# Two transformer blocks on one core: modulation on VectorE in 512-column operations, and another order of loads

## The reference, cut to what matters

```
c_act = jax.nn.silu(c)                                  # one row of 1024
for l in range(2):
    mod = c_act @ w_ada[l] + b_ada[l]                   # 1024 x 3072 weights, one row
    shift, scale, gate = split_cols(mod, (D, D, D))
    h = rms_norm(x, g_pre[l]) * (1.0 + scale) + shift
    (...) = split_cols(h @ w_in[l], IN_SPLITS)          # 1024 x 7328 weights
    # three attentions (8 + 8 + 4x2 heads), gates, output projections: y
    x = x + gate * rms_norm(y, g_post[l])
```

## Time and profile before

| | us |
|---|---|
| median of 3 runs (lowest to highest) | 2483.28 (2481.02 to 2483.42) |
| the profiled execution's own time | 2480.68 |
| its span | 2478.9 |
| TensorE matmul busy | 2309.0 (93%) |
| VectorE busy | 1462.6 (59%) |
| ScalarE busy | 1164.0 (47%) |
| GpSimd busy | 116.6 (5%) |

### The profile page before, as it was taken

How to read it: one execution, slowest core, us unless ns; L and a number is a source line. 1 busy time by engine, 2 the same in 40 slices (tenths; PEclk the granted TensorE clock), 3 DMA queues, 4 the chain that set the end, 5 groups by cost and what they waited for, 6 DMA issues and landing times.

```text
span 2478.9 us, 30332 instructions
## 1 busy us (share of the span) xinstructions
PE 2309.0 (93%) x11596; PEld 1931.6 (78%) x11596; DVE 1462.6 (59%) x1778; ACT 1164.0 (47%) x1416; POOL 116.6 (5%) x61
## 2 busy tenths in 40 slices
PE   6899998889999989999887789999999999999998
PEld 5687677768777878899886668787878787878786
DVE  4311455220145366555543279888888888888886
ACT  0211232121133046443453157777777777767775
POOL 0203322000000012000000000000000000000000
PEclk9999999989999989999898889999999999999999
DMA  9546433444322353355340669998999899999991
GB/s 290 136 137 203 136 103 121 122 102 152 103 85 85 120 156 113 129 194 180 120 148 1 248 219 364 327 367 323 368 324 367 323 371 325 357 339 357 342 351 43
DMA packets 348640, 536.22 MB, mean 216 GB/s; under 512 B 51084, under 2 KB 195392, under 8 KB 348552
## 3 DMA queue, kind: packets, MB, share of 16 engines
q1 hardware_dynamic: 342848, 530.29, 62.3%
q10 hardware_dynamic: 5704, 4.71, 0.6%
HBM read 533.89 MB, written 1.07 MB: 216 GB/s over the span
## 4 chain that ended last, share of the span: by engine, by line
PE 87%; DVE 7%; ACT 3%; issue 1%; DMA 1%; ACTq 0%; POOL 0%; DVEq 0%; SPq 0%
PE bank L561 22%; PE bank L590 17%; PE bank L592 16%; PE bank L591 16%; PE bank L722 2%; PE bank L569 1%; DVE rstd L1733 1%; PE bank L583 1%; PE bank L1107 1%; PE bank L1099 1%; PE bank L651 1%; PE bank L1142 1%; PE bank L686 1%; PE bank L688 1%; PE bank L704 1%
## 5 line engine op out<-in xcount | busy, mean ns | idle before, releaser
L2200 DVE TENSOR_TENSOR w_lo<-pool,w_hi 128x2048 fp32r<-128x2048 f32 x336 | 765.7, 2292 | 134.7 <-ACT w_hi L1622 134.6
L1622 ACT ACTIVATE w_hi<-pool 128x2048 fp32r<-128x2048 f32 x336 | 643.1, 1917 | 147.9 <-PE bank L592 146.3
L561 PE MATMUL bank<-h,ring 128*128 128x256 f32 (+1 forms) x1968 | 448.3, 387 | 11.0 <-DVE h L1835 6.5
L561 PEld LDWEIGHTS bank<-h,ring 128*128 128x128 f32 (+1 forms) x1968 | 373.7, 192 | 81.8 <-issue 24.4
L590 PE MATMUL bank<-w_hi,xe_hi 128*128 128x512 f32 x896 | 359.7, 401 | 4.3 <-DVE w_lo L2200 4.3
L592 PE MATMUL bank<-w_hi,xe_lo 128*128 128x512 f32 x896 | 350.4, 391 | 0.0
L591 PE MATMUL bank<-w_lo,xe_hi 128*128 128x512 f32 x896 | 350.0, 391 | 0.0
L1904 DVE TENSOR_TENSOR piece_lo<-ring,piece_hi 128x1024 fp32r<-128x1024 f32 x118 | 145.2, 1237 | 112.6 <-ACT piece_hi L1263 112.5
L590 PE MATMUL bank<-left_hi,piece_hi 128*128 128x256 f32 x672 | 197.5, 294 | 9.9 <-DVE left_lo L1909 6.2
L590 PEld LDWEIGHTS bank<-w_hi,xe_hi 128*128 128x128 f32 x896 | 168.8, 188 | 45.3 <-DVE w_lo L2200 10.4
L592 PEld LDWEIGHTS bank<-w_hi,xe_lo 128*128 128x128 f32 x896 | 168.7, 188 | 36.3
(11 more groups left out here) (351 smaller groups left out, 2886.7 us busy)
## 6 DMA issues: line engine op xcount, KB each, us to landing
pool<-in_od_exp_w SPq DMA_DIRECT2D x336, 1024.0 KB, 7.0
ring<-in_w_in SPq DMA_DIRECT2D x52, 1024.0 KB, 5.2
ring<-in_ev_ffn_w SPq DMA_DIRECT2D x33, 1024.0 KB, 5.2
ring<-in_w_ada SPq DMA_DIRECT2D x24, 1024.0 KB, 8.4
ring<-in_od_w_in SPq DMA_DIRECT2D x12, 1024.0 KB, 5.4
ring<-in_ev_w_in SPq DMA_DIRECT2D x10, 1024.0 KB, 5.4
ring<-in_w_out SPq DMA_DIRECT2D x8, 1024.0 KB, 5.1
ring<-in_w_in SPq DMA_DIRECT2D x16, 256.0 KB, 4.5
```

What stands on the lines that cost most here:

```text
L561: m = nc.tensor.matmul(b[base:base + rows, 0:cols], left(k), right(k), start=(k == 0), stop=(k == K - 1))
L1622: nc.scalar.activation(w_hi[q % 3], ring_slot(q), ACT.Copy)\
L2200: V.tensor_tensor(w_lo[q % 3], ring_slot(q), w_hi[q % 3].bitcast(F32), ALU.subtract).then_inc(item_vector, tick(item_vector, "lo", q))
```

## The change

- GpSimd computes no modulation any more. `modulation_direct` remains for one unit, (0, 3). The other eleven are VectorE's. It takes both items of a unit in one operation of 2 x 256 = 512 columns where they lie in neighbouring slots of the ring; where they don't (slots 5 and 0), it stays at 256 columns. Each operation waits for the one before it, whose sums it adds to.
- The list begins with units 0, 3, 1, 2 of layer 0 (shift and scale, eight items). The gate units of layer 0 and all of layer 1 lie among layer 0's projections, two items each.
- SyncE no longer waits for the small vectors; identity is fetched ahead of x and has a semaphore of its own.
- ScalarE issues the fetches of biases and tables after the root of layer 0's mean square. Bias lines, lambdas and the bias table's twelve products move in among the projections, on all engines.
- In layer 0, h is x times 1/rms first, then times gain plus shift in one operation.

```diff
-    ADA_ORDER, ADA_VECTOR = (0, 4, 1, 5, 2, 3), 4
-    ADA_AFTER = ("za1", "qb", "zb", "qc")
-    ADA_UNIT = {1: 1, 7: 2, 13: 3, 19: 4}
+    ADA_FIRST, ADA_MATMUL = (0, 3, 1, 2), 3
+    ADA_LATER = [("ckv", 0, 4), ("za1", 0, 5), ("qb1", 1, 0), ("kvb", 1, 1), ("zb1", 1, 2), ("qc1", 1, 3),
+                 ("kc1", 1, 4), ("vc1", 1, 5)]
+    ADA_UNITS = [(0, 0), (0, 1), (0, 2)] + [(l, i) for _, l, i in ADA_LATER]
...
+        pe.wait_ge(consts_set, when(consts_set, "mean"))
+        mean_square(("pre", 0), KD, 1024)
         pe.wait_ge(vecs_ready, when(vecs_ready, "c_act"))
-        modulation_direct(0, 4)
-        pe.wait_ge(loaded_bias, when(loaded_bias, "all"))
-        b = claim("gemm", ("lines",), const_ready, "lines")
-        nc.tensor.matmul(b[0:12, :], rel_bias_sb, onehot_sb, start=True, stop=True)\
-            .then_inc(psum_ready, wrote("lines"))
+        b = claim("gemm", ("mod", 0, ADA_MATMUL), modsum_ready, 0, ADA_MATMUL)
+        for a in range(2):
+            w = take("ada", 0, 2 * ADA_MATMUL + a)
...
         for l in range(L):
             if l == 0:
-                modulation(0, 0)
-                modulation_direct(0, 5)
-                for i in (1, 2, 3):
+                for i in range(3):
                     modulation(0, i)
             release("cq", l)
+            if l == 0:
+                pe.wait_ge(loaded_bias, when(loaded_bias, "all"))
+                b = claim("gemm", ("lines",), const_ready, "lines")
...
             release("ckv", l)
+            if l == 0:
+                pe.wait_ge(consts_set, when(consts_set, "ones"))
+                pe.wait_ge(const_ready, when(const_ready, "lamp"))
+                b = claim("gemm", ("lams",), lame_ready, "lame")
...
             release("ukv", l)
+            if l == 0:
+                modulation(0, 4)
...
+            if l == 0:
+                modulation(0, 5)
+                pe.wait_ge(table_in, when(table_in, "all"))
+                for i in range(12):
+                    b = claim("gemm", ("table", i), table_ready, "table", i)
+                    nc.tensor.matmul(b[:, 0:384], flip, table_up[:, i], start=True, stop=True)\
+                        .then_inc(psum_ready, wrote("table", i))
...
             release("kvb", l)
+            if l == 0:
+                modulation(1, 0)
             for name in ("zb", "qc", "kc", "vc", "zc"):
...
-                if name == "qc" and l + 1 < L:
-                    modulation(l + 1, 0)
+                if l == 0:
+                    modulation(1, 1 + ("zb", "qc", "kc", "vc", "zc").index(name))
...
+        def modulation(l, i):
+            n = ADA_UNITS.index((l, i))
+            if n > 1:
+                dve.wait_ge(psum_ready, when(psum_ready, "mod", *ADA_UNITS[n - 2]))
+            first, second = (where["ada", l, 2 * i + a] for a in range(2))
+            for s in (first, second):
+                dve.wait_ge(slot_loaded[s % RING], loaded_at[s])
+            sums, at = ada_sums[:, n % 2], first % RING
+            beside = at + 1 < RING
+            if beside:
+                both = ring[:, at * SLOT:(at + 2) * SLOT].rearrange("p (a s) -> p a s", a=2)
+            for k in range(KD):
+                if k > 0:
+                    dve.wait_ge(ada_step, ticks.counts["ada_step"])
+                for a in ((slice(0, 2),) if beside else (0, 1)):
+                    w = both[:, :, 256 * k:256 * k + 256] if beside else stream[(first, second)[a]][0][:, k]
+                    if k == 0:
+                        m = V.tensor_scalar(sums[:, a], w, c_act[:, k:k + 1], None, ALU.mult)
+                    else:
+                        m = V.scalar_tensor_tensor(sums[:, a], w, c_act[:, k:k + 1], sums[:, a], ALU.mult, ALU.add)
+                if k < KD - 1:
+                    m.then_inc(ada_step, tick(ada_step))
+            m.then_inc(ada_ready, tick(ada_ready, l, i))
+            for s in (first, second):
+                freed_at[s] = (ada_ready, ticks.counts["ada_ready"])
...
             if l == 0:
+                r = inverse_root("pre", l)
+                for k in range(KD):
+                    m = V.tensor_tensor(h[:, k], x[:, k], r, ALU.mult)
+                modulation(l, 1)
+                modulation(l, 2)
+                shift_gain()
+                for k in range(KD):
+                    V.tensor_scalar(h[:, k], h[:, k], gain[:, k:k + 1], mod[:, k:k + 1], ALU.mult, ALU.add)\
+                        .then_inc(h_ready, tick(h_ready, "pre", l, k))
+                bias_lines()
...
             rotate(("rotk", l), krope, "k", l)
+            if l == 0:
+                lambdas()
+                modulation(0, 4)
             for c in range(2):
                 rotate(("rotq", l, c), qr[:, c], "q", l, c)
+            if l == 0:
+                modulation(0, 5)
+                modulation(1, 0)
+                gate_gain()
+                modulation(1, 1)
             for c in range(4):
                 gate("zb", z["b"][:, c], l, c)
             if l == 0:
                 decay_rates()
+                for i in range(2, 6):
+                    modulation(1, i)
             for c in range(4):
                 gate("zc", z["c"][:, c], l, c)
...
-                    G.tensor_tensor(ada_product, w, c_act.unsqueeze(2).broadcast_to([P, KD, 256]), ALU.mult)\
-                        .then_inc(ada1_step, tick(ada1_step, "product", l, i, a))
...
+        sp.dma_start(ident, C["ident"]).then_inc(ident_in, tick(ident_in, "all", by=16))
         sp.dma_start(xin, A["x"][0].rearrange("(t p) d -> p t d", p=P)).then_inc(x_in, tick(x_in, "x", by=16))
-        sp.dma_start(ident, C["ident"]).then_inc(x_in, tick(x_in, "ident", by=16))
...
-        sp.wait_ge(loaded_rows, when(loaded_rows, "all"))
```

More of the change, by code:

```diff
@@ L398, in two_blocks @@
                     for j in range(2)])
-            if key in ADA_AFTER and l + 1 < L:
-                j = ADA_AFTER.index(key)
-                item(("ada", l + 1, j), cols("w_ada", l + 1, 256 * j, 256 * j + 256))
+            for last, ahead, i in ADA_LATER:
+                if l == 0 and last in (key, key + "1" * (key == "qb")):
+                    for j in (2 * i, 2 * i + 1):
+                        item(("ada", ahead, j), cols("w_ada", ahead, 256 * j, 256 * j + 256))
         for i in range(12):
-            if i % 3 == 0 and l + 1 < L:
-                for j in range(4 + 2 * i // 3, 6 + 2 * i // 3):
-                    item(("ada", l + 1, j), cols("w_ada", l + 1, 256 * j, 256 * j + 256))
             item(("gcols", l, i), cols("w_in", l, 4256 + 256 * i, 4512 + 256 * i))
@@ L754, in _ @@
             if l == 0:
-                modulation(0, 0)
-                modulation_direct(0, 5)
-                for i in (1, 2, 3):
+                for i in range(3):
                     modulation(0, i)
[L759 to L767, removed]
+            else:
+                mean_square(("pre", l), KD, 1024)
             w = take("cq", l)
@@ L770, in _ @@
             release("cq", l)
+            if l == 0:
+                pe.wait_ge(loaded_bias, when(loaded_bias, "all"))
+                b = claim("gemm", ("lines",), const_ready, "lines")
+                nc.tensor.matmul(b[0:12, :], rel_bias_sb, onehot_sb, start=True, stop=True)\
+                    .then_inc(psum_ready, wrote("lines"))
             w = take("ckv", l)
@@ L1709, in _ @@
         dve.wait_ge(vecs_ready, when(vecs_ready, "c_act"))
         modulation(0, 0)
-        modulation(0, 1)
-        b = psum(dve, "lines")
-        dve.wait_ge(loaded_bias, when(loaded_bias, "all"))
-        V.tensor_tensor(lines[0:12, :], b[0:12, :], window_sb, ALU.add)\
-            .then_inc(const_ready, tick(const_ready, "lines"))
-        for l in range(L):
-            for j in range(2):
-                V.tensor_tensor(lamp[0:HEAD, 2 * l + j:2 * l + j + 1], lamv[0:HEAD, 2 * j, l:l + 1],
-                                lamv[0:HEAD, 2 * j + 1, l:l + 1], ALU.mult)\
-                    .then_inc(const_ready, tick(const_ready, "lamp"))
@@ new lines, in lambdas @@
+        def lambdas():
+            dve.wait_ge(lame_ready, when(lame_ready, "lame"))
+            for l in range(L):
+                link(V.tensor_tensor(nlam[:, l:l + 1], lame[:, 2 * l + 1:2 * l + 2], lame[:, 2 * l:2 * l + 1], ALU.subtract))
+                V.tensor_scalar(nlam[:, l:l + 1], nlam[:, l:l + 1], -lam_init(l), None, ALU.add)
+                V.tensor_scalar(gsub[:, l:l + 1], vec("g_sub", l), 1.0 - lam_init(l), None, ALU.mult)\
+                    .then_inc(dve_step, tick(dve_step, "lam"))
```

255 lines of the change are left out of this document (109 added, 146 removed).

## The result

The changed kernel takes 2443.1 us (median of 4 runs, 2442.74 to 2443.87), the kernel before 2483.35 us; the ratio is 0.9849 (95% interval 0.9837 to 0.9861). The profiled execution took 2442.74 us where that of before took 2480.68, 37.9 us less; its span is 2440.9. The forecast was 2443.

The account below looks back on a forecast made before the run. TensorE's path was taken as the bound (87% of what ended last). Start 46 + projections 165.2 + attention units 153.9 = 365.1 instead of 404.4, -39.3 us; forecast 2443, range 2431 to 2459.

Parts of the forecast that it names:

- c_act and the vectors: Start of the kernel: small vectors in at 12.4 us (3 us late beside weight loads), c_act done at 15.6.
- The direct unit: Start, TensorE: unit (0,3), 64 one-column matmuls behind the mean square, takes 13.79 us as before, ending at 35.1.
- the low end: Start: behind the mean square, unit (0,3) could take half its time, h 4.3 us sooner, 2439; 0.68 together with the forecast.
- first projection: End of the start stretch: layer 0's first projection begins at 46 us where it was 80.4, -34.4 us.
- what hides the eight loads is this chain: Start: the 24 us of eight weight loads are covered by the work of TensorE and VectorE in turn.
- A vector unit: One modulation unit on VectorE: 6.1 us in 512-column operations, 7.1 us where 16 operations remain.
- The estimate of 4.8 us a unit: VectorE at 0.59 us per 512-column operation, from the Trainium skill; weighed only, about 3 us less in sum.
- Moved work, 16.0 us: TensorE in layer 0's projections: bias table 8.1 us, lines and lambdas 1.5, eight units' sums 6.4.
- The three holds: TensorE waits in layer 0's projections: q's rotations 2.3 us, qb's load 5.5, kc's load 1.3; 11.0 with slow matmuls.
- 1.9 us of slow matmuls: Layer 0's projections, behind the wait for qb: 32 matmuls take 8.86 us and not 6.95.
- Attention units: Layer 0's 24 attention units take layer 1's 153.9 us instead of 178.3, -24.4 us, with GpSimd idle.
- Rival 4: Layer 0's projections: slower than before, each unit's 14.3 us of free, load, multiply uncovered; all eight give 2546; chance 0.04.

Follow-up runs that it names:

- the repeat: The changed kernel run once more with no edit; median 2438.1 us, four runs from 2428.89 to 2444.85.
- the direct unit first: Changed kernel with modulation unit (0,3), 64 one-column matmuls, placed ahead of the mean square on TensorE; 2449.7 us.
- Unit (0,4) early and decay later: Changed kernel with VectorE's unit (0,4) moved ahead of za's gates and the 24 decay operations moved behind unit (1,3); 2414.3 us, ratio 0.9736.

## Why the prediction was right, and where not

**c_act and the vectors: right.** 12.7 and 15.9 us for 12.4 and 15.6. In the second two errors cancelled: the vectors were copied by 13.9 and not 14.9, and I had not counted the 1.28 us of ScalarE's table load, which now stands in the open. That part is luck.

**The direct unit: mis-sized.** "Direct unit (0,3): 13.79 us": it took 9.14, 11.55 in the repeat. I had named this as the low end and taken the row of before, in which TensorE came out of an idle. The run with the direct unit first gives 13.78 back and shows that its place, not its work, decides. The 4.6 us didn't all arrive, because the load of unit (0,2) ended at 33.5: **first projection at 42.8 instead of 46, 3.2 us better than forecast**, 1.6 to 2.1 better in the profiles with the longer direct unit (43.9 to 44.4). That "what hides the eight loads is this chain" was nearly wrong: the chain and the loads are of equal length.

**A vector unit: right** (6.0 for 6.1, 7.0 for 7.1). The estimate of 4.8 us a unit, worked out from the Trainium skill, "VectorE: DVE Perf Modes", section on the TRN2 errata, was rightly refused: the units measured are 1.2 us longer. The same section says that this row of its table is too low for single operations and gives (N+151)/0.96 ns for one with two fp32 inputs, 0.69 us at 512 columns, which agrees with the 0.68 us of the earlier trace rows.

**Moved work, 16.0 us: right.** Unit (0,4) early and decay later leaves 14.9 over layer 1.

**The three holds: right in place and size, wrong in what follows one.** 2.5, 4.9, 1.8 for 2.3, 5.5, 1.3. But behind them I charged 1.9 us of slow matmuls, and they cost 1.7 at L791, 0.8 at the sum and 2.7 in qb, 5.2 together: slow matmuls began already at the 1.9 us wait for q's rotations. The run with unit (0,4) early and decay later has none of the holds, and prices them: 168.2 - 153.1 = 15.1 us where I had 11.0, of which 8.1 are waits and 7.0 TensorE's busy time (155.8 against 148.7). This is the term that took the projections to 168.2 instead of 165.2; the moved work gave 1.1 of it back.

**Attention units: right.** 155.5 for 153.9; the 1.6 us are one gate block at 5.41 us instead of 3.72 near the start of the units (granted clock 0.68 from 213.5 to 218.9), absent in the two profiles with 153.8 and 153.9. That it is GpSimd was an inference from layer 1; taking GpSimd's work out of the kernel before, and putting idle work into the one after, has now shown it from both sides. Rival 4 did not come: TensorE waits for VectorE at none of the eight sums among the projections.

**The sum.** -37.6, +22.5, -22.8 against -34.4, +19.5, -24.4: -37.9 against -39.3. Two misses of 3 us, of opposite sign, made the total better than its parts. The forecast of the median to 0.1 us is luck: the changed kernel can draw 2430 as well as 2443, and I didn't know of that.

## What to carry to other kernels

When an idle engine takes work off a busy one, look at what they share: 64 us of GpSimd "for nothing" cost 17 us of the attention units, 11.4 as waits of TensorE and 5.5 as slower matmuls, and twin stages of the same program with and without it showed that before any experiment. In a ring that is loaded in order, ask of every item who frees its slot and when that engine gets to it: moving one 6 us unit to where its engine idled was worth 12 us. Compare two profiles only after asking which draws of the clock each of them had. And charge a wait of TensorE with the slow matmuls behind it, not with its own length alone.

## What the runs showed of the hardware that I had not expected

- The same program draws one of two lengths, 12 to 16 us apart; the profiles put 11 us of it on TensorE's granted clock in one 550 us stretch (0.92 against 0.95). The kernel before never drew the shorter one in the 24 runs of it that the comparisons use (2477.8 to 2484.9), while without GpSimd's work it ran 12 to 15 us shorter in four of five (2438.3 to 2440.7 against 2453.1); why, is open.
- One-column matmuls, which take as long as their weights' load (9.14 and 9.27 us for the 64), follow the clock too: eight take 0.95 us at the full level and 1.84 at half, and 64 take 13.78 us out of an idle, 8.6 to 11.6 behind 5.3 to 6.6 us of wide matmuls. The clock also fell to half while TensorE did nothing but these, without a gap (at 26 us of the changed kernel).
- A GpSimd fill, which reads nothing, lengthens VectorE's scaling with one SBUF input from 350 to 462 ns and a two-input operation of two columns from 153 to 299, but neither its wide two-input one (481) nor its reduction from SBUF (686).
